# Expert layers of a two-block network: 64 of 256 tokens take their chosen table rows by indirect transfers, the dense products run over the other 192

## The chip, the cores and the metric

The kernel runs on one core of one Trainium2 chip. The metric is the device time of one execution in microseconds (us), lower is better. All data and sums are float32; large products split each operand into a high part (rounded to the matmul's input format) and a low part (what is left), and add three of the four partial products.

## What is computed

```python
def _peer(x, wq, k1, k2, u_tab, v_tab):
    # 8 heads, product keys (2 x 128 sub-keys), top 16 per half, 256 candidates, final top 16, softmax
    q = (xt @ wq).reshape(T, PEER_HEADS, 2, PEER_DQ_HALF)
    s1 = jnp.einsum('thd,nd->thn', q[:, :, 0], k1); s2 = jnp.einsum('thd,nd->thn', q[:, :, 1], k2)
    v1, i1 = lax.top_k(s1, 16); v2, i2 = lax.top_k(s2, 16)
    cand = (v1[..., :, None] + v2[..., None, :]).reshape(T, PEER_HEADS, 256)
    cidx = (i1[..., :, None] * 128 + i2[..., None, :]).reshape(T, PEER_HEADS, 256)
    sc, pos = lax.top_k(cand, 16)
    eidx = jnp.take_along_axis(cidx, pos, axis=-1).reshape(T, 128)
    gate = jax.nn.softmax(sc, axis=-1).reshape(T, 128)
    ub = jnp.take(u_tab, eidx, axis=0)                       # 16384 x 1024 table
    act = gelu(jnp.einsum('td,tkd->tk', x, ub))
    vb = jnp.take(v_tab, eidx, axis=0)                       # 16384 x 1024 table
    return jnp.einsum('tk,tkd->td', gate * act, vb)
```

There are 256 tokens of width 1024. A first block of two layers (FFN, hybrid mixer, FFN) comes first and is untouched; then two layers of a mixer and this expert layer, each followed by a layer norm. Each token chooses 8 x 16 = 128 of 16,384 experts.

## The kernel before, in words

Everything is one hand-written program per engine; the order in each is written out, and engines meet at semaphores only. All weights come as one stream of 944 units of 128 x 1024 floats (512 KB each). SyncE (SP) loads unit n into one of three slots of `ring` as soon as unit n-3 has been split (`load`, L497). ScalarE (ACT) writes the high half of a unit to `wsp` and VectorE (DVE) the low half (`Splitter.one`, L446: L454 and L457); TensorE (PE) then uses it.

An expert layer (`peer` in each engine's program) goes through these stages:

- Queries and scores: 16 units, then 8 heads x 2 halves of scores for each block of 128 tokens. Block 0's scores stay in PSUM (`ACC`), block 1's are copied to `sc1`.
- **U stage**, 128 units. Unit j holds the rows of the first table whose first sub-key is j. `product_unit` (L714) makes 24 matmuls, each with a 128 x 128 piece of the table as the stationary operand and the 256 tokens moving; ACT takes the gelu (L1758), giving for each expert and token an activation. Block 0's activations stay in `arena`; block 1's are spilled to DRAM (`act_out`, L513).
- During the first 92 units (`U_FIRST`) DVE picks the experts: `first_choice` (top 16 of 128, twice a head), `pair_sums`, `second_choice` (top 16 of 256), `places`, `look_up`, `less_the_first`, `gates_of` (softmax), between which it puts its own low halves one at a time (`low_next`). GpSimd (POOL) makes 18 of the low halves (`POOL_LOWS`, L680) at the start, while DVE chooses for four heads of block 0. ACT takes the exponentials after units 19, 39 and 76 (`EXP_AT`); for each it stops until DVE has sent the scores, and no high half is made meanwhile.
- The gates of block 0's tokens go by scatter: POOL issues 128 indirect transfers (L688) that add 128 gates each into a cleared DRAM buffer, `second_dram`. The 32 groups of four tokens of block 1 (`GROUPS`) go by one-hots: DVE makes two one-hot matrices and two scaled ones (L2645, L2654), PE multiplies them (L1342, 8 matmuls a group) and ACT copies the result into `arena` (L1807). `groups_behind` puts one group behind each unit from 93 on.
- **V stage**, 128 units. SP fetches the spilled row j from DRAM (`second_back`, L527), DVE multiplies it with `arena` (`gate`, L2671), ACT and DVE split the product (L1789, L2676) and `down_unit` (L777) makes 12 matmuls with 512 columns moving: 2 blocks of tokens x 3 partial products x 2 halves of the width, summed in four PSUM banks.
- The layer norm adds the four banks to `h`, block 0 first.

DVE's program in one round of the V stage, in order: `gate(j + 1)`, `low(j)`, the low half of unit j+1.

Of the kernel before, what the change touches and what calls it, by code (L numbers as in the profile page):

```python
# [13 lines left out]
F32 = mybir.dt.float32  # L14
# [7 lines left out]
P = 128  # L22
D = 1024
# [19 lines left out]
U_FIRST = 92  # L43
POOL_LOWS = 18
EXP_AT = (19, 39, 76)
ZEROED = 16
# [3 lines left out]
GROUPS = P // 4  # L50
ROUND = 16 * TOPK
# [34 lines left out]
PEER_STAGES = [("xT", 8, 0), ("tt", 16, 16), ("score", 4, 0), ("U", U_FIRST, U_FIRST), ("selT", 1, 0),  # L86
# [3 lines left out]
def groups_behind(q):  # L90

    return min(GROUPS, max(0, q - U_FIRST))

# [21 lines left out]
def build_program(nc, x, stream, consts, consts1, levels, p1, p2, swt, wa, wgu, rows1, rows2, rows3, out):  # L115
    ctx = ExitStack()
    with ctx:
# [9 lines left out]
        arena = at("arena", 0, [P, NKEYS * T])  # L127
        ysp = at("ysp", 0, [P, 2, 4, T], F32R)
        scratch = at("scratch", 0, [P, NKEYS * T])
        place = 4 * NKEYS * T  # L130
# [15 lines left out]
        selT = at("selT", place + 8192 + 4 * 1280, [P, 4, P], F16)  # L146
        acts = at("acts", place + 8192 + 4 * 1536, [P, 4, P])
# [7 lines left out]
        spots = at("spots", place + 2048, [P, HK], U32)  # L155
# [178 lines left out]
        second_dram = [nc.dram_tensor(f"second_dram{l}", (NKEYS * P * T, 1), F32, kind="Internal").ap() for l in range(DEPTH)]  # L334
        second_rows = [d.rearrange("(j p t) o -> j p (t o)", j=NKEYS, p=P) for d in second_dram]
        row_dram = [nc.dram_tensor(f"row_dram{l}", (4, T), F32, kind="Internal").ap() for l in range(DEPTH)]
        rows_out = sem("rows_out")
        bm_in = sem("bm_in")
        zeroed = sem("zeroed")
        scattered = sem("scattered")  # L340
# [7 lines left out]
        gated = sem("gated")  # L348
        high_done = sem("high_done")
# [139 lines left out]
        def _(sp):  # L489
# [2364 lines left out]
```

## Time and profile before

| | us |
|---|---|
| median of 3 runs (2989.09 to 2989.77) | 2989.67 |
| the profiled execution | 2988.89 |
| its span | 2986.9 |
| PE busy in the span | 2928.5 |
| DVE busy | 2124.6 |
| ACT busy | 1498.2 |
| POOL busy | 680.0 |

Times in the trace are counted from the start of the span. The second expert layer's U stage starts at 2237.06 and its V stage at 2626.11; the first one's at 1325.26 and 1714.19. "Idle before" an instruction is the time that its engine stood still ahead of it. A time in brackets with an arrow in a timeline is such a wait and what ended it. In the timelines a row may merge several instructions: its count is behind the x, its second number the time from the first one's start to the last one's end. Engine SPq is SyncE's queue of transfers. PEld is the weight load that goes ahead of each matmul. In a windows row the columns are: length, then busy time and number of instructions of PE, PEld, DVE, ACT and POOL, the granted clock of PE (1.00 is 2.4 GHz), the busy share of the 16 DMA engines and GB/s.

### The profile page before, as it was taken

How to read it: one execution, taken by the hardware profiler on the slowest of the kernel's cores; microseconds unless marked ns; L12 is line 12 of the kernel's file. 1: busy time of each engine (PE TensorE's matmuls, PEld its weight loads, DVE VectorE, ACT ScalarE, POOL GpSimd, SP SyncE). 2: the span in 40 equal slices, each digit the busy share in tenths (PEclk: the TensorE clock that was granted, in tenths of full speed). 3: DMA queues.
4: the chain of work that ended last, by engine and by line, in shares of the span. 5: the costliest groups of instructions: out<-in, count | busy, mean ns of one | idle time of the engine just before them, and what ended most of it. 6: DMA issues, size and time to landing. Idle time of an engine off the chain costs nothing.

```text
span 2986.9 us, 54746 instructions
## 1 busy us (share of the span) xinstructions
PE 2928.5 (98%) x18452; PEld 2598.6 (87%) x18452; DVE 2124.6 (71%) x3656; ACT 1498.2 (50%) x2410; POOL 680.0 (23%) x443
## 2 busy tenths in 40 slices
PE   8999999999999999999999999999999999999998
PEld 7888888888878888899999988888899999988887
DVE  6667566766766667758986677777758996767776
ACT  4455444444554445445555544455545555554544
POOL 0002100000021002117877400000207877500000
PEclk9998999999999999999999999999999999999999
DMA  6545455555473554457887677776446888777775
GB/s 222 190 161 180 153 167 186 174 183 189 148 233 113 184 187 152 157 173 199 198 211 189 176 247 262 243 240 203 163 163 191 196 209 197 176 235 266 239 244 189
DMA packets 255982, 581.52 MB, mean 195 GB/s; under 512 B 61336, under 2 KB 127168, under 8 KB 255344
## 3 DMA queue, kind: packets, MB, share of 16 engines
q1 hardware_dynamic: 210656, 547.94, 56.8%
q0 software_dynamic: 45200, 31.93, 6.9%
q8 instruction: 76, 1.25, 0.2%
q14 instruction: 50, 0.41, 0.0%
HBM read 542.92 MB, written 36.84 MB: 194 GB/s over the span
## 4 chain that ended last, share of the span: by engine, by line
PE 81%; DVE 10%; ACT 4%; issue 2%; DMA 2%; POOL 1%; SPq 0%; DVEq 0%; ACTq 0%
PE acc L785 31%; PE work L721 26%; PE work L731 9%; PE work L733 5%; DVE wsp L457 4%; PE acc L1205 2%; PE acc L849 2%; ACT wsp L454 2%; DMA ring<-in_stream 2%; PE acc L1342 1%; ACT scratch L1421 1%; PE work L1127 0%; POOL st L584 0%; DVE scratch L2033 0%; PE work L1242 0%
## 5 line engine op out<-in xcount | busy, mean ns | idle before, releaser
L457 DVE TENSOR_TENSOR wsp<-ring,wsp 128x1024 fp32r<-128x1024 f32 x908 | 1105.2, 1225 | 568.7 <-ACT wsp L454 564.4
L454 ACT ACTIVATE wsp<-ring 128x1024 fp32r<-128x1024 f32 x944 | 984.9, 1052 | 506.1 <-PE work L721 251.8
L721 PE MATMUL work<-xsp,wsp 128*128 128x256 f32 x7872 | 971.7, 285 | 6.2 <-DVE wsp L457 3.2
L721 PEld LDWEIGHTS work<-xsp,wsp 128*128 128x128 f32 x7872 | 953.8, 192 | 11.2 <-DVE wsp L457 4.5
L785 PE MATMUL acc<-wsp,hsp 128*128 128x512 f32 x4128 | 955.4, 390 | 6.6 <-DVE hsp L2676 4.7
L785 PEld LDWEIGHTS acc<-wsp,hsp 128*128 128x128 f32 x4128 | 767.8, 188 | 171.1 <-issue 4.4
L731 PE MATMUL work<-xsp,wsp 128*128 128x512 f32 x1408 | 503.7, 400 | 6.5 <-DVE xsp L1861 5.0
L688 POOL DMA_INDIRECT second_dram<-rows_sb,spots x256 | 465.8, 1819 | 148.4 <-issue 90.8
L733 PE MATMUL work<-xsp,wsp 128*128 128x256 f32 x1408 | 395.8, 281 | 0.0
L731 PEld LDWEIGHTS work<-xsp,wsp 128*128 128x128 f32 x1408 | 265.4, 188 | 74.6 <-DVE xsp L1861 6.1
L584 POOL TENSOR_TENSOR st<-st,mhalf 128x1 f32<-128x1 f32 x24 | 20.6, 862 | 1356.4 <-DVE st L1881 805.0
L1789 ACT ACTIVATE hsp<-arena 128x256 fp32r (+1 forms) x256 | 107.0, 418 | 336.4 <-PE acc L785 322.7
L733 PEld LDWEIGHTS work<-xsp,wsp 128*128 128x128 f32 x1408 | 266.7, 189 | 3.1
L2676 DVE TENSOR_TENSOR hsp<-arena,hsp 128x256 fp32r<-128x256 f32 x256 | 108.8, 425 | 60.1 <-ACT hsp L1789 60.0
L1456 ACT ACTIVATE hsp<-scratch 128x256 fp32r<-128x256 f32 x88 | 36.8, 418 | 218.4 <-DVE scratch L1954 218.4
L1448 ACT ACTIVATE scratch<-scratch 128x256 f32<-128x256 f32 x88 | 36.8, 418 | 188.1 <-DVE scratch L1944 188.1
L680 POOL TENSOR_TENSOR wsp<-ring,wsp 128x1024 fp32r<-128x1024 f32 x36 | 89.7, 2492 | 130.6 <-ACT wsp L454 130.4
L2671 DVE TENSOR_TENSOR arena<-arena,back 128x256 f32 (+1 forms) x256 | 107.2, 419 | 10.5 <-ACT arena L1807 6.0
L849 PE MATMUL acc<-wsp,xsp 128*128 128x512 f32 x384 | 100.8, 413 | 0.0
L1205 PE MATMUL acc<-wsp,xsp 128*128 128x512 f32 x384 | 93.9, 397 | 0.0
L849 PEld LDWEIGHTS acc<-wsp,xsp 128*128 128x128 f32 x384 | 72.9, 197 | 16.2
L1205 PEld LDWEIGHTS acc<-wsp,xsp 128*128 128x128 f32 x384 | 70.3, 188 | 15.3
(355 smaller groups left out, 2138.1 us busy)
## 6 DMA issues: line engine op xcount, KB each, us to landing
ring<-in_stream SPq DMA_DIRECT2D x944, 512.0 KB
back<-second_dram SPq DMA_DIRECT2D x256, 128.0 KB, 3.2
second_dram<-back POOLq DMA_DIRECT2D x32, 512.0 KB, 13.3
second_dram<-arena SPq DMA_DIRECT2D x184, 64.0 KB
rows_sb<-in_rows POOLq DMA_DIRECT2D x10, 512.0 KB, 6.4
second_dram<-acts SPq DMA_DIRECT2D x72, 64.0 KB
second_dram<-rows_sb,spots POOLq DMA_INDIRECT x256
h_saved_dram<-h POOLq DMA_DIRECT2D x2, 1024.0 KB, 5.0
```

Source lines behind the costliest of these rows:

```text
L454: self.eng.activation(dst[:, 0, :], src, ACT.Copy).then_inc(high_done, 1)
L457: self.eng.tensor_tensor(dst[:, 1, :], src, dst[:, 0, :].bitcast(F32), ALU.subtract)\
L688: pool.indirect_dma_start(out=second_dram[l], in_=selv[:, 0, 2, n:n + 1], in_offset=None, out_offset=bass.IndirectOffsetOnAxis(spots[:, n: ...
L721: mm = pe.matmul(out_, lhsT=w[:, a, 128 * c:128 * c + 128], rhs=xsp[:, b, c, :], start=(c == 0 and n == 0), stop=(c == DC - 1 and n == 2))
L731: pe.matmul(out_, lhsT=w[:, 0, 128 * c:128 * c + 128], rhs=xcs[:, c, :, :].rearrange("p s t -> p (s t)"), start=(c == 0), stop=False)
L733: mm = pe.matmul(out_[:, 0:T], lhsT=w[:, 1, 128 * c:128 * c + 128], rhs=xsp[:, 0, c, :], start=False, stop=(c == DC - 1))
L785: mm = pe.matmul(ACC[2 * b + n][:, :], lhsT=act[:, pa, 128 * b:128 * b + 128], rhs=w[:, pw, 512 * n:512 * n + 512], start=(first and m == ...
L849: mm = pe.matmul(ACC[2 * (g % 2) + b][:, :], lhsT=xsp[:, px, c, 128 * b:128 * b + 128], rhs=w[:, pw, 512 * cc:512 * cc + 512], start=(c == ...
L1205: mm = pe.matmul(ACC[2 * (g % 2) + b][:, :], lhsT=xsp[:, px, c, 128 * b:128 * b + 128], rhs=w[:, pw, 512 * cc:512 * cc + 512], start=(c == ...
L1789: act.activation(hsp[:, j % 2, 0, :], arena[:, bass.ds(it * (6 * T) + j * T, T)], ACT.Copy)\
L2671: tt(a, a, back[j % 4], ALU.mult).then_inc(gated, 1)
L2676: tt(hsp[:, j % 2, 1, :], arena[:, bass.ds(it * (12 * T) + j * T, T)], hsp[:, j % 2, 0, :].bitcast(F32), ALU.subtract).then_inc(act_low, 1)
```

## The change

Of block 1's 128 tokens the last 64 are taken out of the dense products. For each of them, 64 rows at a time on each half of the 128 partitions, POOL fetches the chosen rows of the first table by indirect transfers from a copy of it in row order (`urows`, a new input), DVE takes the inner product of each row with the token's `h` (a `scalar_tensor_tensor` with a sum, L2663), ACT takes the gelu, DVE multiplies with the gates, POOL fetches the rows of the second table (straight from the stream) and DVE adds each, scaled, to a sum (L2684). A partition holds one of the 64 tokens and 64 of its 128 experts: 64 transfers of 128 rows x 4 KB for each table and layer, through 6 slots. At the end PE adds the two halves with a small matrix, `fold`.

The other 192 tokens (`TD`): the U products are 192 columns wide and all activations are spilled. All gates of the 192 go by one-hots, 48 groups in place of 32, five groups behind every two units from unit 61 on; the scatter and the clearing of its buffer go. POOL makes the low halves of 69 units in place of 18, and DVE none during the choice. In a V unit the 64 tokens of block 1 that are left have their high and low parts side by side as 128 stationary columns: 4 matmuls for them (all four partial products) and 6 for block 0, 10 in place of 12.

```diff
-U_FIRST = 92
-POOL_LOWS = 18
-EXP_AT = (19, 39, 76)
+U_FIRST = 60
+POOL_LOWS = 69
+DOTS_FROM = 76
+EXP_AT = (19, 36, 56)
-GROUPS = P // 4
+GROUPS = (T - 64) // 4
+FETCHED = 64
+TD = T - FETCHED
+PAIRS_OF = TOPK // 2
+SLOTS = 6
+ROWS = PH * PAIRS_OF
+AHEAD = 4
+COEF_AT = (106, 127)
 def groups_behind(q):
-    return min(GROUPS, max(0, q - U_FIRST))
+    return min(GROUPS, max(0, 5 * (q - U_FIRST) // 2))
+def dots_behind(q):
+    return min(ROWS, max(0, ROWS * (q - DOTS_FROM) // (NKEYS - 2 - DOTS_FROM)))
...
 # POOL
-                pool.wait_ge(zeroed, 16 * ZEROED * (l + 1))
-                for i in range(PH):
-                    ...
-                        pool.indirect_dma_start(out=second_dram[l], in_=selv[:, 0, 2, n:n + 1], in_offset=None,
-                                                out_offset=bass.IndirectOffsetOnAxis(spots[:, n:n + 1], 0),
-                                                compute_op=ALU.add).then_inc(scattered, 16)
+                def fetch(n):
+                    m = n % ROWS
+                    k = TOPK * (m // PAIRS_OF) + m % PAIRS_OF
+                    if 2 * ROWS * l + n >= SLOTS:
+                        pool.wait_ge(row_used, 2 * ROWS * l + max(n - SLOTS + 1, 0))
+                    table, which = (urows, 0) if n < ROWS else (value_rows, 1)
+                    pool.indirect_dma_start(out=fetched[:, n % SLOTS, :], out_offset=None, in_=table,
+                                            in_offset=bass.IndirectOffsetOnAxis(gidx[:, which, k:k + 1], 0))\
+                        .then_inc(row_in[n % SLOTS], 16)
...
+                for n in range(2 * ROWS):
+                    fetch(n)
...
 # PE, U stage
-                        product_unit(G, q, G.bank(q)[:, 0:T], it * UNITS_BODY)
+                        product_unit(G, q, G.bank(q)[:, 0:TD], it * UNITS_BODY, n_=TD)
 # PE, value_unit
-                    down_unit(G, i, hsp[:, i % 2, :, :], first, last, 6 * n)
+                    for m in range(2):
+                        for n in range(2):
+                            mm = pe.matmul(ACC[2 + n][:, :], lhsT=both[:, 2 * P:2 * TD], rhs=w[:, m, 512 * n:512 * n + 512],
+                                           start=(first and m == 0), stop=(last and m == 1))
+                    ...
+                    for m, n in order:
+                        pa, pw = PARTS[m]
+                        mm = pe.matmul(ACC[n][:, :], lhsT=act[:, 0:P, pa], rhs=w[:, pw, 512 * n:512 * n + 512],
+                                       start=(first and m == 0), stop=(last and m == 2))
...
+                pe.wait_ge(row_used, 2 * ROWS * (l + 1))
+                for n in range(2):
+                    pe.wait_ge(packed_out, 2 * l + n + 1)
+                    c = slice(512 * n, 512 * n + 512)
+                    pe.matmul(ACC[2 + n][:, :], lhsT=fold[:, 64:192], rhs=row_total[:, c], start=True, stop=False)
+                    mm = pe.matmul(ACC[2 + n][:, :], lhsT=fold[:, 0:P], rhs=packed[:, c], start=False, stop=True)
...
 # DVE
+                def dots(n):
+                    for _ in range(n):
+                        m = taken[0]
+                        r = row(m)
+                        ...
+                        stt(r, r, 1.0, xrow, ALU.mult, ALU.mult, accum_out=coef[:, m:m + 1]).then_inc(row_used, 1)
+                        taken[0] += 1
...
-                for q in range(U_FIRST + 1, NKEYS - 2):
+                for q in range(U_FIRST + 1, NKEYS):
                     for g in range(groups_behind(q - 1), groups_behind(q)):
                         if g + 1 < GROUPS:
                             one_hot(g + 1)
                         gate_parts(g)
-                    split.upto(U.u + q + 1)
+                    if q < NKEYS - 2:
+                        if split.next == U.u + 3 + POOL_LOWS and U.u + q + 1 >= split.next:
+                            dve.wait_ge(low_done, split.next)
+                        split.upto(U.u + q + 1)
+                    dots(dots_behind(q) - taken[0])
...
+                coefficients(0)
+                for m in range(AHEAD):
+                    add_row(m)
...
                     for j in range(2, 14):
                         gate(j + 1, it)
                         low(j, it)
                         split.one(V.u + j + 1, it, 12)
+                        if j % 2:
+                            add_row(AHEAD + (j - 3) // 2, it)
```

DVE where the one-hots begin, behind the last unit of the choice. Before, one group stands ahead of each low half:

```order
L2632 MEMSET st 128x1
L2645 TENSOR_TENSOR one_hots<-iota_65,selT 128x512 x4
L2654 TENSOR_TENSOR one_hots<-one_hots,selT 128x512 x2
L457 TENSOR_TENSOR wsp<-ring,wsp 128x1024
L2645 TENSOR_TENSOR one_hots<-iota_65,selT 128x512 x2
L2654 TENSOR_TENSOR one_hots<-one_hots,selT 128x512 x2
L457 TENSOR_TENSOR wsp<-ring,wsp 128x1024
```

In the changed kernel the same place reads:

```order
L2755 MEMSET st 128x1
L2769 TENSOR_TENSOR one_hots<-iota_71,selT 128x512 x4
L2778 TENSOR_TENSOR one_hots<-one_hots,selT 128x512 x2
L2769 TENSOR_TENSOR one_hots<-iota_71,selT 128x512 x2
L2778 TENSOR_TENSOR one_hots<-one_hots,selT 128x512 x2
L2769 TENSOR_TENSOR one_hots<-iota_71,selT 128x512 x2
L2778 TENSOR_TENSOR one_hots<-one_hots,selT 128x512 x2
```

DVE's low halves are gone from between the groups; while these 27 groups run, POOL makes them.

POOL from the saving of `h` on. Before, it makes 18 low halves in six rounds of three and then issues the scatter:

```order
L680 TENSOR_TENSOR wsp<-ring,wsp 128x1024
L676 REGISTER_ALU
L676 COMPARE_AND_BRANCH
L688 DMA second_dram<-rows_sb,spots 4194304x1 x128
L694 DMA h<-h_saved_dram 128x2048
```

In the changed kernel 23 rounds come first, and all transfers wait behind them:

```order
L710 TENSOR_TENSOR wsp<-ring,wsp 128x1024
L706 REGISTER_ALU
L706 COMPARE_AND_BRANCH
L731 DMA gidx<-gidx 64x4x8 x4
L736 DMA fgate<-fgate 64x4x8 x2
L723 DMA fetched<-in_urows,gidx 128x1024 x64
L723 DMA fetched<-in_stream,gidx 128x1024 x25
L742 DMA h<-h_saved_dram 128x2048
L723 DMA fetched<-in_stream,gidx 128x1024 x39
```

No indirect transfer writes DRAM any more, and 128 now write SBUF.

DVE in two units of the V stage of the changed kernel, where each unit had `arena<-arena,back`, `hsp<-arena,hsp` and `wsp<-ring,wsp` before:

```order
L2799 TENSOR_TENSOR arena<-arena,back_61 128x192
L2803 REGISTER_ALU
L2804 TENSOR_TENSOR gsp<-arena,gsp 128x192
L491 REGISTER_ALU
L492 TENSOR_TENSOR wsp<-ring,wsp 128x1024
L2797 REGISTER_ALU
L2799 ISA
L2799 TENSOR_TENSOR arena<-arena,back_87 128x192
L2803 REGISTER_ALU
L2804 TENSOR_TENSOR gsp<-arena,gsp 128x192
L491 REGISTER_ALU
L492 TENSOR_TENSOR wsp<-ring,wsp 128x1024
L2679 REGISTER_ALU
L2684 ISA
L2684 SCALAR_TENSOR_TENSOR xrow<-fetched,coef,xrow 128x1024
```

The last row is the addition of a fetched row, behind every second unit.

## Rows read from the trace of the kernel before

**Rows 1.** The page: busy time by engine, and the chain that ended last.

```profile
PE 2928.5 (98%) x18452; PEld 2598.6 (87%) x18452; DVE 2124.6 (71%) x3656; ACT 1498.2 (50%) x2410; POOL 680.0 (23%) x443
...
PE 81%; DVE 10%; ACT 4%; issue 2%; DMA 2%; POOL 1%; SPq 0%; DVEq 0%; ACTq 0%
```

**Rows 2.** Windows: the first 92 units of the second U stage; 200 us of V.

```profile
2237.06:2499.60 262.54, 260.91 (x2163) 259.77 (x2162) 218.49 (x512) 136.49 (x195) 201.83 (x104) 1.00 0.77 198
...
2750.00:2950.00 200.00, 200.00 (x884) 165.60 (x883) 146.28 (x221) 100.11 (x147) 0.00 (x0) 1.00 0.73 242
```

**Rows 3.** Timeline of PE: U stage, V stage and next stage of the first layer begin.

```profile
1325.26 4.92 PE L721 MATMUL work<-xsp,wsp 128*128 128x256 f32 x39
...
1714.19 2.00 PE L785 MATMUL acc<-wsp,hsp 128*128 128x512 f32 x8
...
2066.20 1.07 PE L743 MATMUL work<-xsp 128*128 128x512 f32 x4
```

**Rows 4.** Timelines of PEld and PE: trains of weight loads and matmuls; one group by shape.

```profile
234.50 1.86 PEld L897 LDWEIGHTS work<-cst,scratch 128*128 128x128 f32 x16
...
L897 PE MATMUL work<-cst,scratch 128*128 128x1 f32 x64 | 7.4, 245 | 0.0
...
1325.23 4.86 PEld L721 LDWEIGHTS work<-xsp,wsp 128*128 128x128 f32 x40
...
2849.83 6.96 PE L785 MATMUL acc<-wsp,hsp 128*128 128x512 f32 x30
...
1664.23 0.63 PE L1342 MATMUL acc<-one_hots 128*128 128x128 f16 x8
```

**Rows 5.** Timeline of DVE in the choice beside POOL's lows (layer 2); durations of L2504, L680.

```profile
2238.07 0.30 DVE L2474 MAX8 topv<-acc 128x8 f32<-128x128 f32 x1 [5.29 <-ACT scores L1751]
...
2239.93 0.30 DVE L2474 MAX8 topv<-acc 128x8 f32<-128x128 f32 x1
...
2256.45 0.43 DVE L2474 MAX8 rows_sb<-rows_sb 128x8 f32<-128x256 f32 x1
...
2258.97 0.43 DVE L2474 MAX8 rows_sb<-rows_sb 128x8 f32<-128x256 f32 x1
...
2281.91 2.28 DVE L2564 TENSOR_SCALAR spots<-rows_sb,pr 128x64 uint32<-128x64 f32 x1
...
L2504 DVE TENSOR_TENSOR rows_sb<-topv x8: 1218/1219/3476, 1341.1 to 2418.3; 128x1024 f32<-128x1024 f32 x8
...
L680 POOL TENSOR_TENSOR wsp<-ring,wsp x36: 2394/2401/2873, 1329.6 to 2290.4; 128x1024 fp32r<-128x1024 f32 x36
```

**Rows 6.** Timeline of ACT at the third exponential.

```profile
2460.99 1.28 ACT L1763 ACT_TABLE_LOAD   x1
2462.28 0.31 ACT L1763 ACTIVATE rows_sb<-rows_sb 128x128 f32<-128x128 f32 x1
...
2463.90 1.06 ACT L454 ACTIVATE wsp<-ring 128x1024 fp32r<-128x1024 f32 x1
```

**Rows 7.** Timeline of DVE and ACT: one group of one-hots in the first layer.

```profile
1664.90 0.76 DVE L2645 TENSOR_TENSOR one_hots<-iota,selT 128x512 f16<-128x512 f16 x2 [0.83 <-PE acc L1342]
...
1665.58 0.75 DVE L2654 TENSOR_TENSOR one_hots<-one_hots,selT 128x512 f16<-128x512 f16 x2
```

**Rows 8.** Timeline of DVE in one unit of the V stage.

```profile
2850.84 1.23 DVE L457 TENSOR_TENSOR wsp<-ring,wsp 128x1024 fp32r<-128x1024 f32 x1 [0.53 <-ACT wsp L454]
...
2851.98 0.42 DVE L2671 TENSOR_TENSOR arena<-arena,back 128x256 f32 x1
...
2852.61 0.43 DVE L2676 TENSOR_TENSOR hsp<-arena,hsp 128x256 fp32r<-128x256 f32 x1 [0.21 <-ACT hsp L1789]
```

**Rows 9.** Windows with much DMA; durations of the indirect transfers' issue and of L2332.

```profile
5.00:10.00 5.00, 2.26 (x11) 2.29 (x12) 3.11 (x7) 3.45 (x9) 3.28 (x5) 1.00 1.04 409
...
2722.00:2742.00 20.00, 20.00 (x89) 16.33 (x87) 12.91 (x19) 8.63 (x13) 1.73 (x3) 1.00 0.89 311
...
L688 POOL DMA_INDIRECT second_dram<-rows_sb,spots x256: 1537/1581/2631, 1390.3 to 2595.1; - x128
...
L2332 DVE SCALAR_TENSOR_TENSOR h<-h,st,rows_sb x10: 1279/1282/1286, 1155.4 to 2981.2; 128x1024 f32<-128x1024 f32 x10
```

More of the change, by code:

```diff
@@ L348, in build_program @@
         gated = sem("gated")
+        xrow_in = sem("xrow_in")
+        rows_moved = sem("rows_moved")
+        gates_moved = sem("gates_moved")
+        row_in = [sem(f"row_in{i}") for i in range(SLOTS)]
+        row_used = sem("row_used")
+        packed_out = sem("packed_out")
         high_done = sem("high_done")
@@ L671, in _ @@
                 pool.wait_ge(h_saved, 16 * (l + 1))
+                for half in range(2):
+                    pool.dma_start(xrow[64 * half:64 * half + 64, :], saved[64:P, 1, :]).then_inc(xrow_in, 16)
                 U = Group(f"peer{l}", "U")
@@ new lines, in _ @@
+                for half in range(2):
+                    i = half * (PH // 2)
+                    pool.wait_ge(ev("rows_known"), 2 * l + half + 1)
+                    for w in range(2):
+                        pool.dma_start(first_half(gidx[0:64, w, :], i), second_half(gidx[64:P, w, :], i)).then_inc(rows_moved, 16)
+                pool.wait_ge(rows_moved, 64 * (l + 1))
+                pool.wait_ge(ev("sel_ready"), 3 * l + 2)
+                for half in range(2):
+                    i = half * (PH // 2)
+                    pool.dma_start(first_half(fgate[0:64, :], i), second_half(fgate[64:P, :], i)).then_inc(gates_moved, 16)
@@ L1767, in activate_all @@
                     rounds = (last - first) // UNITS_BODY
-                    with act.Fori(0, rounds) as it:
-                        for q in range(first, first + UNITS_BODY):
-                            activate(q, it)
+                    if rounds > 1:
+                        with act.Fori(0, rounds) as it:
+                            for q in range(first, first + UNITS_BODY):
+                                activate(q, it)
+                    else:
+                        rounds = 0
                     for q in range(first + rounds * UNITS_BODY, last):
@@ L1819, in peer @@
                     split.upto(G.u + j + 1)
+                act.wait_ge(ev("packed_done"), l + 1)
+                act.wait_ge(row_used, 2 * ROWS * (l + 1))
+                for n in range(2):
+                    act.activation(packed[:, 512 * n:512 * n + 512], ACC[2 + n][:, :], ACT.Copy).then_inc(packed_out, 1)
                 split.upto(G.u + 129)
@@ L2606, in peer @@
                 for half in range(2):
-                    low_next()
                     pair_sums(half)
                     for i in range(PH // 2 * half, PH // 2 * (half + 1)):
-                        low_next()
-                        second_choice(1, i, low_next if i % 2 else None)
-                    if half == 0:
-                        for i in range(PH // 2, PH):
-                            for m in range(2):
-                                low_next()
-                                first_choice(1, i, m)
```

216 lines of the change are left out of this document (138 added, 78 removed).

## The prediction

> **What bounds the kernel now.** I read the page first: PE is busy 98% of the span and stands for 81% of the chain that ended last [rows 1]. The windows tell the stages apart [rows 2]: in the first 92 units of U, PE and its weight loads are both full (260.9 and 259.8 of 262.5 us) and POOL and DVE have work most of the time; in V, PE is full while DVE has 146 of 200 us and the DMA engines 0.73 of their time, at 242 GB/s. So before the change PE sets both stages, and the question is what stands right behind it. In the first layer U takes 1325.26 to 1714.19, 388.9 us, and V from there to 2066.20, 352.0 us [rows 3].
>
> Rates of PE come from trains of equal instructions, their time less one instruction's, over their number less one [rows 4]. A U matmul (256 columns) starts every (4.86 - 0.19) / 39 = 0.120 us, so a unit of 24 takes 2.88. A V matmul (512 columns) starts every (6.96 - 0.39) / 29 = 0.2265, so a unit of 12 takes 2.72. A one-hot group of 8 takes, from (0.63 - 0.22) / 7, 0.06 each and some 0.52 in all with its joints.
>
> **The change part by part**, per expert layer.
>
> *(a) Units 0 to 59.* The U matmuls go from 256 to 192 columns. That would be 0.09 us if columns were all, but in [rows 4] the 16 matmuls of one column behind 128-column weight loads still start every (1.86 - 0.19) / 15 = 0.111 us. So a unit costs between 24 x 0.111 = 2.67 and the 2.88 of now; I take 2.67, as the weight load is the same. The Trainium skill ("TensorE: Matmul & The Clock Gate", section "LDWEIGHTS (loading the stationary operand)") gives columns / 1.2 ns, 107 ns for 128, which would make it 2.56; the trace is near it, a little above.
>
> That gain isn't had, because DVE is late. Its choice is on the way: ACT stops after unit 56 until DVE has sent the last scores, and makes no high half meanwhile. Prices from [rows 5]: `first_choice` 2239.93 - 2238.07 = 1.86, `second_choice` 2258.97 - 2256.45 = 2.52; the first four heads of block 0 with all around them, beside POOL's low halves, 2238.07 to 2284.19 = 46.1. In these, some DVE instructions take over 2 us longer than alone: L2504 takes 1.22 alone and 3.48 beside an L680, whose own length is 2.40, and L2564 2.28. DVE waits there for POOL's instruction to end. Now POOL makes 69 low halves, so all of the choice is priced that way. The two halves of block 0 cost 46.1 and one more conversion of 2.3 each (the second index), 96.8. Block 1: 16 x 1.86 + 8 x 2.52 + 2 x 3.5 (L2504) = 57.0, and the look-ups: in the half above they are 46.1 - 14.9 - 10.1 - 3.5 - 2.3 = 15.3, with the same instructions at twice the size here, between 15 and 30, taken as 17 since most of it is waiting. Three softmaxes about 1 each. With a start at 1.0 the scores are sent at 175. Then a table load, the exponential, a table load, a high half (1.28 + 0.31 + 1.28 + 1.06 [rows 6]) and POOL's low half 2.40: unit 59 starts at 181, unit 60 at 184. Before it started at 60 x 2.88 = 172.8. **+11 us.** If the 17 is 30, or if DVE is not held up at all, this is +24 or -7 (60 units of 2.67 and the exponential).
>
> *(b) Units 60 to 79.* All 48 groups fall here, 2.5 a unit. A group takes DVE four instructions in (0.76 + 0.75), 1.51 us [rows 7]: 72.4. DVE's own low halves of the units from 72 on cost 1.14 each (L457 starts, L2671 starts 1.14 later [rows 8]): 8 x 1.14 = 9.1. Three inner products, 1.24 each (L2332 is of that form, 1.28 [rows 9]): 3.7. The transposed choice and the start 4. That is 89, against PE's 20 x 2.67 + 48 x 0.52 = 78. Until unit 71 POOL still makes low halves, nine of 2.40 = 21.6 us. No row of before shows a one-hot beside one. If they go side by side it costs nothing; if they exclude each other, all 21.6. I take all, by the row that is nearest, L2504, also a `tensor_tensor` with both inputs in SBUF. 111, against 20 x 2.88 = 57.6: **+53**, down to +32.
>
> The Trainium skill ("SBUF — State Buffer", section "Who interferes with whom") says that a DVE instruction with two SBUF inputs and a GpSimd instruction that reads SBUF exclude each other for a whole instruction. L2504's row agrees.
>
> *(c) Units 80 to 127 and the handover.* PE has 48 x 2.67 = 128. DVE has 48 low halves and 61 inner products, 48 x 1.14 + 61 x 1.24 = 130. The DMA engines: the fullest window moves 409 GB/s at a share of 1.04 [rows 9], so 512 KB cost at least 1.28 us. 48 loads and 61 fetches (each 128 rows of 4 KB, 512 KB) are 139.5, the spills of 96 KB 0.24 each, 11.5: 151 us. So here the transfers set the pace. POOL's issue takes 1.6 (up to 2.6) with 0.3 between [rows 9], 61 x 2.1 = 128, hidden. At the end DVE has the last inner products and four row additions (4 x 1.2, each waiting for a fetch) ahead of the low half of unit 127; PE has two units of work in hand, so some 9 us are lost. 160, against 48 x 2.88 + 32 x 0.52 = 154.9: **+5**.
>
> *(d) V.* PE's unit becomes 10 x 0.2265 = 2.27. DVE per unit: 1.14 for the low half, 0.28 and 0.28 for the two instructions of 192 columns (0.42 at 256, which start 0.33 apart, less a quarter of the streaming), and half a row addition of 1.2: 2.30. The DMA engines: 1.5 x 1.28 + 0.24 for the row read back = 2.16. Three resources stand within 6% of each other, and DVE, which waited 0.53 and 0.21 for ACT in each unit of before [rows 8], has no slack left to take a wait. The floor is 2.30, the ceiling what (c)'s slower DMA would give, 2.75. I take 2.50, a third of DVE's waits back. 128 x (2.50 - 2.72): **-28**.
>
> *(e) Ends.* Four matmuls of `fold`, plain float32 of 512 columns, between 0.45 and 0.9 each (two instructions, in one or two passes), behind two copies by ACT that hide under the last unit; six more transposes. **+4**, 2 to 6. The scatter and the clearing of its buffer lay beside PE's work: 0; the 1 to 3 us that they could hide aren't in the sum.
>
> Sum: 11 + 53 + 5 - 28 + 4 = +45 a layer, **+90 us**. Against the profiled execution's 2988.9 this is **3079**; the median of the runs, 2989.7, lies 0.8 above it. A measurement of this kernel can tell 0.2%, some 6 us, from no change.
>
> **The rivals.**
> - *V at its floor, DVE and POOL side by side* (faster). (a) -7, (b) +32, (c) +5, (d) 128 x (2.30 - 2.72) = -54, (e) +4: -20 a layer, 2949. It decides where DVE's wait for POOL doesn't come with the one-hots and a V unit is under 2.45. For it: PE was the only full engine in V. Against it: L2504's row. 0.12.
> - *V at its floor, the waits as forecast.* 11 + 53 + 5 - 54 + 4 = +19: 3027. 0.18.
> - *Side by side, V at 2.50.* +6 a layer: 3001. 0.10.
> - *Transfers slower than their best.* The only window in which POOL's queue moves megabytes beside the stream shows 311 GB/s at 0.89 [rows 9], 350 when full: 512 KB in 1.50. (c) 109 x 1.50 + 48 x 0.28 + 9 = 186, +31; V 2.75, +4: 103 a layer, 3195. 0.15.
> - The forecast, 0.45.
>
> **How the numbers follow.** Faster by over 0.2% is the first rival, 0.12, and a hundredth for what I don't see. Within 0.2% 0.02. Slower, the rest, 0.85. The range leaves out the first rival and goes up to the last: 2990 to 3195. The slower cases are near enough to each other that they need no range of their own.
>
> **What would show it.** In the changed profile: U matmuls 0.111 apart in the first units; ACT idle ahead of the third exponential for over 10 us, ended by DVE, and PE idle with it; from unit 61 to 71 one-hot instructions of over 2 us beside POOL's low halves, and units of 6 us; DMA share near 1 from unit 80 on, DVE waiting for fetched rows, units of 3.1 us; V units of 2.3 to 2.75. U in all 455 us (184 + 111 + 160), V 320. I am wrong if U takes under 420, which would mean that DVE and POOL don't hold each other up, or if V units stay above 2.72.

## The result, and the profile after

The changed kernel takes 3172.9 us (median of 4 runs, 3162.6 to 3185.5), the one before 2989.4: a ratio of 1.0616, 95% interval 1.0571 to 1.0661, or +183.5 us. The forecast was +90 and 3079. The direction and the range (2990 to 3195) hold, the size is off by a factor of two. The profiled execution took 3166.1, its span is 3164.3.

The page of the changed kernel, busy time by engine and the chain that ended last, as in [rows 1]:

```profile
PE 2901.0 (92%) x18218; PEld 2535.7 (80%) x18218; DVE 2364.2 (75%) x4093; ACT 1482.7 (47%) x2364; POOL 801.7 (25%) x528
...
PE 44%; DMA 17%; DVE 16%; issue 10%; POOL 7%; ACT 6%; DVEq 1%; SPq 0%; POOLq 0%; ACTq 0%
```

PE's busy time fell by only 27 us, and PE no longer makes up the chain: it was 81% of it, now 44%. The windows tell where. Five stretches of the first expert layer (columns as in [rows 2]):

```profile
1321.28:1500.20 178.92, 166.22 (x1449) 164.83 (x1447) 156.69 (x451) 84.62 (x129) 145.99 (x59) 0.96 0.67 202
1500.20:1550.00 49.80, 36.34 (x282) 34.63 (x280) 37.41 (x67) 17.23 (x30) 19.41 (x8) 0.76 0.34 102
1550.00:1624.70 74.70, 60.47 (x577) 57.38 (x577) 62.36 (x146) 32.76 (x59) 17.26 (x17) 0.89 0.48 149
...
1700.00:1791.16 91.16, 71.34 (x587) 69.07 (x587) 72.10 (x96) 33.28 (x54) 48.53 (x37) 0.93 1.03 403
...
1900.00:2050.00 150.00, 131.31 (x532) 101.82 (x531) 122.23 (x184) 73.06 (x107) 40.09 (x30) 0.98 0.93 322
```

In the second and third stretch, units 60 to 79, no engine is full, and PE's clock is down. In the fourth the DMA engines are full. In the last, in V, PE, DVE and the DMA engines are all at 0.8 to 0.93, and none is full.

The places where the stages begin, in the timeline of PE:

```profile
1321.28 70.17 PE L769 MATMUL work<-xsp,wsp 128*128 128x192 f32 x624
1392.18 62.90 PE L769 MATMUL work<-xsp,wsp 128*128 128x192 f32 x552 [0.73 <-POOL wsp L710]
...
1494.28 5.36 PE L769 MATMUL work<-xsp,wsp 128*128 128x192 f32 x24 [11.09 <-POOL wsp L710]
...
1500.22 5.60 PE L769 MATMUL work<-xsp,wsp 128*128 128x192 f32 x48
...
1624.69 2.90 PE L769 MATMUL work<-xsp,wsp 128*128 128x192 f32 x24 [0.59 <-DVE wsp L492]
...
1791.16 1.94 PE L1409 MATMUL acc<-wsp,gsp 128*128 128x512 f32 x4
...
2150.57 1.02 PE L1434 MATMUL acc<-xrow,fold 128*128 128x512 f32 x2
...
2153.60 5.15 PE L791 MATMUL work<-xsp 128*128 128x512 f32 x20
```

The first row holds 26 units in 1392.18 - 0.73 - 1321.28 = 70.2, 2.70 a unit. 1500.22 is the start of unit 60, 1624.69 that of unit 80, 1791.16 that of V, 2150.57 that of the fold. The stages, in us a layer:

| | forecast | first layer | second layer |
|---|---|---|---|
| units 0 to 59 | 184 | 178.9 | 181.2 |
| units 60 to 79 | 111 | 124.5 | 123.2 |
| units 80 to 127 and handover | 160 | 166.5 | 164.1 |
| V | 320 | 359.4 | 357.7 |
| fold | 4 with all else | 3.0 | 3.4 |

The first layer takes 2153.60 - 1321.28 = 832.3 where it took 740.9 [rows 3]: +91.4, and twice that is the result. The forecast had +45. To set its terms against the measured ones, the stages of the kernel before have to be read from the same trace, by counting PE's matmuls: units 0 to 59 took 176.0, units 60 to 79 57.7, units 80 to 127 155.2 and V 352.0. The sum of the prediction goes from 172.8, 57.6, 154.9 and 348.2 (128 x 2.72), 7 us less in all, so its stage times (779 with the fold) lie 53 below the 832 and its difference 46 below the +91. In differences, for the first layer:

| | forecast | measured | missing |
|---|---|---|---|
| units 0 to 59 | +11 | +2.9 | -8 |
| units 60 to 79 | +53 | +66.8 | +14 |
| units 80 to 127 and handover | +5 | +11.3 | +6 |
| V | -28 | +7.4 | +35 |
| fold | +4 | +3.0 | -1 |

So V is 35 of the 46 us a layer that the forecast lacked: it was to give 28 back and costs 7 more. Units 60 to 79 are 14, and the other three nearly cancel.

### The profile page after: what moved, and what is told of

Read it like the earlier page. It is cut to its first block, busy times and chain, and to the rows that moved or that the text cites. A ratio compares the mean times of both kernels' runs of the same rounds, so it can differ in the third digit from the quotient of the medians.

```text
span 3164.3 us, 54654 instructions
## 1 busy us (share of the span) xinstructions
PE 2901.0 (92%) x18218; PEld 2535.7 (80%) x18218; DVE 2364.2 (75%) x4093; ACT 1482.7 (47%) x2364; POOL 801.7 (25%) x528
## 4 chain that ended last, share of the span: by engine, by line
PE 44%; DMA 17%; DVE 16%; issue 10%; POOL 7%; ACT 6%; DVEq 1%; SPq 0%; POOLq 0%; ACTq 0%
DMA ring<-in_stream 16%; PE acc L833 9%; PE work L779 9%; PE work L769 9%; POOL wsp L710 6%; DVE wsp L492 6%; PE work L781 5%; ACT wsp L489 4%; PE acc L1253 2%; PE acc L897 2%; PE acc L1416 2%; DVE one_hots L2778 2%; DVE one_hots L2769 2%; PE acc L1409 1%; DVE fetched L2663 1%
## 5 line engine op out<-in xcount | busy, mean ns | idle before, releaser
L769 PE MATMUL work<-xsp,wsp 128*128 128x192 f32 (+1 forms) x7872 | 966.9, 284 | 88.2 <-DVE wsp L492 59.6
L1416 PE MATMUL acc<-wsp,gsp 128*128 128x512 f32 x1536 | 411.6, 404 | 0.0
L710 POOL TENSOR_TENSOR wsp<-ring,wsp 128x1024 fp32r<-128x1024 f32 x138 | 340.6, 2475 | 243.5 <-ACT wsp L489 243.2
L781 PE MATMUL work<-xsp,wsp 128*128 128x256 f32 x1408 | 395.8, 281 | 0.0
L1409 PE MATMUL acc<-wsp,gsp 128*128 128x512 f32 x1024 | 293.5, 409 | 82.9 <-DVE gsp L2804 82.5
L1416 PEld LDWEIGHTS acc<-wsp,gsp 128*128 128x128 f32 x1536 | 305.5, 199 | 63.8
L1409 PEld LDWEIGHTS acc<-wsp,gsp 128*128 128x128 f32 x1024 | 190.7, 193 | 156.8 <-issue 114.8
L723 POOL DMA_INDIRECT fetched<-in_stream,gidx x128 | 183.5, 1434 | 458.3 <-DVE xrow L2684 429.9
L833 PE MATMUL acc<-wsp,hsp 128*128 128x512 f32 x1056 | 256.8, 392 | 1.9 <-DVE hsp L2047 1.9
L833 PEld LDWEIGHTS acc<-wsp,hsp 128*128 128x128 f32 x1056 | 191.9, 188 | 44.3 <-DVE hsp L2047 3.6
L723 POOL DMA_INDIRECT fetched<-in_urows,gidx x128 | 172.2, 1345 | 217.9 <-DVE fetched L2663 200.2
L2684 DVE SCALAR_TENSOR_TENSOR xrow<-fetched,coef,xrow 128x1024 f32<-128x1024 f32 x126 | 161.2, 1279 | 4.2 <-DMA fetched<-in_stream,gidx 4.0
L2663 DVE SCALAR_TENSOR_TENSOR fetched<-fetched,xrow 128x1024 f32<-128x1024 f32 x128 | 153.7, 1218 | 0.0
```

The costliest lines, as they stand in the source:

```text
L710: pool.tensor_tensor(dst[:, 1, :], ring[:, n % RING, :], dst[:, 0, :].bitcast(F32), ALU.subtract) .then_inc(low_done, 1)
L723: pool.indirect_dma_start(out=fetched[:, n % SLOTS, :], out_offset=None, in_=table, in_offset=bass.IndirectOffsetOnAxis(gidx[:, which, k:k ...
L769: mm = pe.matmul(out_, lhsT=w[:, a, 128 * c:128 * c + 128], rhs=xsp[:, b, c, 0:n_], start=(c == 0 and n == 0), stop=(c == DC - 1 and n == 2))
L781: mm = pe.matmul(out_[:, 0:T], lhsT=w[:, 1, 128 * c:128 * c + 128], rhs=xsp[:, 0, c, :], start=False, stop=(c == DC - 1))
L833: mm = pe.matmul(ACC[2 * b + n][:, :], lhsT=act[:, pa, 128 * b:128 * b + 128], rhs=w[:, pw, 512 * n:512 * n + 512], start=(first and m == ...
L1409: mm = pe.matmul(ACC[2 + n][:, :], lhsT=both[:, 2 * P:2 * TD], rhs=w[:, m, 512 * n:512 * n + 512], start=(first and m == 0), stop=(last an ...
```

## The experiments

The table has the stages of each run's profiled execution, mean of the two layers, and the run's median time. The ratio's interval is given with each. Executions of the changed kernel and its variants scatter more than those of the kernel before (23 us between four of the changed kernel), and the profiled one is not always near the median: with 60 low halves on POOL it is the slowest of five, 3143.5.

| kernel | units 60 to 79 | 80 to 127 | V, a unit | us |
|---|---|---|---|---|
| changed | 124 | 165 | 2.80 | 3172.9 |
| second table's fetches small | 122 | 169 | 2.50 | 3085.0 |
| the same by plain transfers | 121 | 167 | 2.76 | 3152.7 |
| row additions narrow | 121 | 168 | 2.68 | 3136.7 |
| 60 low halves on POOL | 103 | 170 | 2.81 | 3121.3 |
| first table's fetches small | 122 | 143 | 2.80 | 3121.2 |
| small fetches, narrow additions | 123 | 167 | 2.39 | 3061.5 |
| idle matmuls ahead of groups | 124 | 168 | 2.79 | 3179.5 |
| groups and products spread | 69 | 172 | 2.80 | 3079.2 |
| spread, addition first | 71 | 175 | 2.93 | 3105.0 |
| spread, weights' low half first | 72 | 174 | 3.08 | 3151.5 |
| spread, gates one further ahead | 70 | 174 | 2.87 | 3090.0 |

Theory after the result: V is paced by the loop of the three ring slots. A load can start only when DVE has made the low half of the unit three before it, and now it lands later, since a fetch is in flight beside it. The rival is DVE, with a row addition in every second unit. The chain of waits of the changed kernel in V, a piece of it (start, us, what):

```profile
1861.02 6.02 DMA ring<-in_stream
1867.06 1.07 ACT wsp L489
...
1869.29 0.47 DVE xrow L2684
...
1870.49 0.35 DVE arena L2799
1870.84 0.27 DVE gsp L2804
1871.11 1.15 DVE wsp L492
1872.42 6.43 DMA ring<-in_stream
1878.87 1.07 ACT wsp L489
```

In the 1872.42 - 1861.02 = 11.4 us from one load's start to the other's, SP starts four loads, so this is four units of 2.85; 6.0 of them pass until the load has landed, and the rest is one high half and what DVE does up to the second low half behind it. That this loop sets the pace is a reading of the chain. The experiments below test it.

**1. Small fetches in V.**

```diff
-pool.indirect_dma_start(out=fetched[:, n % SLOTS, :], out_offset=None, in_=table,
+w = D if n < ROWS + SLOTS else 32
+if w == 32:
+    table = stream.rearrange("n p (a d) -> (n p a) d", d=32)
+pool.indirect_dma_start(out=fetched[:, n % SLOTS, 0:w], out_offset=None, in_=table,
```

> The second table's fetches, all but a layer's first six, move 128 bytes a row and not 4 KB (so 16 KB and not 512 KB each; the rows are then not the chosen ones and only 32 of 1024 columns of them are fresh). All instructions of the engines stay. Theory 'transfers': the V stage is paced by the loop of three ring slots, whose load lands later because a fetch is in flight beside it. Then the load lands within 4.5 us and a V unit falls from 2.80 us to what DVE takes, 2.3 to 2.5: V 295 to 320 us a layer, the kernel about 3060 to 3100. Rival 'DVE': the row additions make DVE late. Then V stays at 345 us or more a layer and the kernel above 3150.

Measured: 3085.0, ratio 1.0306 (1.0286 to 1.0327); V 318.9 and 320.7 a layer, 2.50 a unit. Windows of V:

```profile
1900.00:2050.00 150.00, 146.28 (x608) 115.55 (x607) 141.03 (x213) 82.50 (x123) 41.08 (x30) 0.99 0.80 258
2900.00:3050.00 150.00, 146.13 (x607) 115.15 (x606) 140.95 (x215) 81.19 (x121) 40.74 (x30) 0.99 0.82 265
```

DVE is now at 0.94 and PE at 0.97, and the chain's loads land in 4.35 to 4.73 us in place of 5.4 to 7.2. So the bytes of the fetches cost 0.30 us a unit, 39 us a layer. What is left, 2.50, is what the forecast took for V with the fetches in it.

**2. The same bytes by plain transfers.**

```diff
+if n >= ROWS:
+    pool.dma_start(fetched[:, n % SLOTS, :], stream[n]).then_inc(row_in[n % SLOTS], 16)
+    return
```

> Each fetch of the second table is replaced by one plain transfer of the same 512 KB from the stream, from the same queue into the same slot (other rows, the same bytes and semaphores). If V is paced by the bytes that the transfers share, nothing moves: 3160 to 3185. If it is the form of the fetches (one row per descriptor at scattered addresses, and GpSimd's 1.4 us of issue), a V unit falls towards that of the run with small fetches, and the kernel under 3130.

Measured: 3152.7, ratio 1.0545 (1.0523 to 1.0567), V 2.76 a unit. It is 20 us below the changed kernel, a little outside what was expected for "bytes", and far from the 3130 of "form". So the bytes make nearly all of it. The 0.04 of 0.30 a unit that would be the form's is hardly clear of the scatter of the runs.

**3. Row additions on 32 columns.**

```diff
-ins = stt(row_total, fetched[:, s, :], c, row_total, ALU.mult, ALU.add)
+ins = stt(row_total[:, 0:32], fetched[:, s, 0:32], c, row_total[:, 0:32], ALU.mult, ALU.add)
```

> The row additions of the V stage work on 32 of 1024 columns (the sum over the fetched rows is left out for the rest); all transfers stay. DVE sheds 60 x about 1.1 us a layer. Theory 'transfers': a V unit stays within 0.15 of 2.80 us, the kernel 3130 to 3175. Rival 'DVE': a V unit falls to PE's 2.27 to 2.4, V to 290 to 307 us a layer, and the kernel to 3050 to 3070.

Measured: 3136.7, ratio 1.0482 (1.0458 to 1.0506), V 2.68 a unit. DVE fell from 122 to 102 of 150 us, and the DMA share rose to 0.96. So DVE's load alone isn't the bound: with the additions all but gone and the fetches as they were, V stays above 2.6. The additions cost 0.12 a unit.

**4. Sixty low halves on POOL** (`POOL_LOWS = 60`, was 69).

> POOL makes the low halves of 60 units in place of 69, DVE those from unit 63 on. Theory 'POOL and DVE exclude each other in the one-hots': nine low halves of 2.40 us on POOL that hold DVE up become nine of 1.14 on DVE, so units 60 to 79 fall from 124 us by 8 to 15 a layer, and no one-hot takes over 2 us from unit 63 on: the kernel 3140 to 3160. Rival 'it is PE's lower clock after its idle time and the ping-pong with the one-hots': units 60 to 79 stay within 5 us of 124, the kernel 3165 to 3185. Rival 'side by side': DVE gets nine more instructions, +10 a layer, 3190.

Measured: 3121.3, ratio 1.0445 (1.0427 to 1.0462). Units 60 to 79 take 102.1 and 104.8. What an instruction of the one-hots takes there, in the changed kernel:

```profile
L2778 DVE TENSOR_TENSOR one_hots<-one_hots,selT x94: 406/418/2604, 1504.5 to 1623.0; 128x512 f16<-128x512 f16 x94
```

and with 60 low halves on POOL:

```profile
L2778 DVE TENSOR_TENSOR one_hots<-one_hots,selT x94: 407/415/448, 1507.0 to 1603.6; 128x512 f16<-128x512 f16 x94
```

The longest falls from 2604 to 448 ns when POOL's low halves are gone. In the changed kernel's first layer POOL makes ten low halves behind unit 60's start; each has just one long one-hot instruction beside it, which ends 0.3 us after it: the first, which starts in the middle of POOL's, is 1.81 us long, the others are 2.56 to 2.63. The exclusion of the two engines is shown. Nine low halves moved from POOL to DVE are worth 20 us a layer, more than the 8 to 15 expected, and the kernel is faster than expected too. These 20 are not all DVE's: its busy time in the stretch falls by 10 only (99.8 to 90.0 in the first layer), and PE's granted clock rises with it, from 0.76 and 0.89 to 0.95:

```profile
1505.00:1605.00 100.00, 84.31 (x850) 79.95 (x849) 88.15 (x212) 47.81 (x85) 12.59 (x15) 0.95 0.50 155
```

**5. Small fetches of the first table.** The edit of experiment 1, for `SLOTS <= n < ROWS` and on `urows`.

> The first table's fetches, all but a layer's first six, move 128 bytes a row and not 4 KB (other rows, and only 32 of 1024 columns fresh); everything else as changed. Theory 'transfers' of the prediction: units 80 to 127 with the handover (166 us a layer in the changed kernel, DMA share 1.0) fall to what DVE takes, 130 + 9 to 150: the kernel 16 to 27 us a layer faster, 3120 to 3145. Rival 'DVE and PE, coupled through two shallow buffers': this stretch stays at 160 or more, the kernel above 3155. V stays at 2.80 a unit in both.

Measured: 3121.2, ratio 1.0443 (1.0419 to 1.0467). Units 80 to 127 take 143.2 and 142.7 in place of 165. The window from 1630 to 1780:

```profile
1630.00:1780.00 150.00, 138.05 (x1182) 136.02 (x1180) 136.38 (x189) 64.32 (x106) 115.83 (x66) 0.95 0.84 252
```

The bytes of the fetches cost 22 us in this stretch, so the transfers were its bound. Behind them stand PE and DVE, both at 0.9, and POOL's issuing, which is 49% of the chain of waits there: so 143 is not DVE's own pace.

**6. Both of V's costs away** (edits 1 and 3).

> Small second-table fetches and row additions on 32 columns together. With the transfers gone alone a V unit took 2.49, with the additions gone alone 2.68. If PE is the next bound, 2.27 to 2.35 a unit, V 290 to 300 us a layer, the kernel 3040 to 3060. If something else is in the loop (ACT, the fetch of the spilled row, the ring of three slots), it stays above 2.40, V above 307, the kernel above 3065.

Measured: 3061.5, ratio 1.0239 (1.0222 to 1.0256), V 2.39 a unit. PE in V:

```profile
1952.28 1.08 PE L1412 MATMUL acc<-wsp,gsp 128*128 128x512 f32 x4
1953.19 1.56 PE L1419 MATMUL acc<-wsp,gsp 128*128 128x512 f32 x6
1954.59 1.08 PE L1412 MATMUL acc<-wsp,gsp 128*128 128x512 f32 x4
```

Between 1900 and 2050 PE never waits (busy 150.0 of 150), and a unit takes 1954.59 - 1952.28 = 2.31. So PE is the bound, at 2.31 in an undisturbed stretch and 2.39 over the whole stage, a little above the 2.35 that was expected of PE; 10 x 0.2265 was 2.27. The row of six starts its matmuls (1.56 - 0.39) / 5 = 0.234 apart, against 0.2265 in [rows 4].

**7. Idle matmuls ahead of each group.** In the changed kernel units 60 to 79 show something that was not in the forecast. Timelines of PE, then of DVE and POOL:

```profile
1510.93 1.03 PE L1394 MATMUL acc<-one_hots 128*128 128x128 f16 x8 [2.86 <-DVE one_hots L2778]
1511.72 5.16 PE L769 MATMUL work<-xsp,wsp 128*128 128x192 f32 x24
...
1521.82 5.23 PE L769 MATMUL work<-xsp,wsp 128*128 128x192 f32 x24
```

```profile
1504.38 2.38 POOL L710 TENSOR_TENSOR wsp<-ring,wsp 128x1024 fp32r<-128x1024 f32 x1 [1.14 <-ACT wsp L489]
1504.45 2.93 DVE L2778 TENSOR_TENSOR one_hots<-one_hots,selT 128x512 f16<-128x512 f16 x2
...
1507.05 2.53 POOL L710 TENSOR_TENSOR wsp<-ring,wsp 128x1024 fp32r<-128x1024 f32 x1 [0.30 <-ACT wsp L489]
1507.30 2.90 DVE L2769 TENSOR_TENSOR one_hots<-iota,selT 128x512 f16<-128x512 f16 x2
...
1517.39 0.76 DVE L2769 TENSOR_TENSOR one_hots<-iota,selT 128x512 f16<-128x512 f16 x2 [3.84 <-PE acc L1394]
```

POOL makes DVE late, PE stands still 2.86 us for DVE, then runs its next 24 matmuls in 5.16 us and not 2.90 (the lower of its clock's two levels; the window's mean is 0.76), and DVE in turn stands still 3.84 us for PE, since only three groups' one-hots fit. The edit gives PE work in its idle time:

```diff
+for _ in range(3):
+    pe.matmul(ACC[g % 4][:, :], lhsT=xsp[:, 0, 6, 0:128],
+              rhs=xcs[:, 4, :, :].rearrange("p s t -> p (s t)"), start=True, stop=True)
 pe.wait_ge(oh_ready, n + 1)
```

The wait for the group's bank, which stood behind `oh_ready`, goes ahead of both.

> PE makes three idle 512-column matmuls of 0.2265 us ahead of each one-hot group (into the group's own bank, overwritten after), 33 us a layer of PE work with no use, where it waits for DVE anyway. If PE's lower clock after its idle time costs time in units 60 to 79, the granted clock there rises from 0.76 to 0.89 to above 0.95, the 24 matmuls of a unit take 2.9 and not 5.2 us, and the stretch falls from 124 us to 110 to 120 in spite of the added work. If DVE, held up by POOL, sets it alone, it stays within 4 of 124. If PE is the bound, it rises to 135 or more.

Measured: 3179.5, ratio 1.0648 (1.0626 to 1.0669), and 124.2 in both layers for units 60 to 79:

```profile
1500.00:1550.00 50.00, 44.79 (x360) 39.11 (x360) 39.86 (x78) 18.57 (x31) 20.98 (x9) 0.91 0.38 121
1550.00:1624.00 74.00, 71.04 (x629) 60.75 (x629) 56.38 (x131) 31.63 (x54) 18.55 (x16) 1.00 0.44 135
```

The clock rose to 0.91 and 1.00 (above 0.95 was expected), the time did not fall. The 33 us of added work a layer cost nothing, but PE is then nearly full itself (71.0 of 74.0), so the run doesn't say how much the lower clock cost. That stays open.

**8. Groups and inner products spread over the stage.**

```diff
-POOL_LOWS = 69
-DOTS_FROM = 76
+POOL_LOWS = 60
+DOTS_FROM = 64
-    return min(GROUPS, max(0, 5 * (q - U_FIRST) // 2))
+    return min(GROUPS, max(0, q - U_FIRST))
```

> One one-hot group behind each unit from 61 to 108 in place of five behind every two, the inner products from unit 65 on in place of 77, and POOL makes 60 low halves in place of 69. DVE has 48 groups of 1.51, 65 low halves of 1.14 and 64 inner products of 1.24 = 226 us behind unit 60, PE 68 x 2.67 + 48 x 0.52 = 207. If DVE's total is what bounds the second half of U, units 60 to 127 take 230 to 250 us a layer where the kernel with 60 low halves on POOL took 273, and the kernel 3060 to 3100. If it is the coupling inside each unit, 260 or more, and the kernel 3110 or more.

Measured: 3079.2, ratio 1.0308 (1.029 to 1.0325). Units 60 to 127 take 241 and 242 a layer, where they took 291 and 287 in the changed kernel and 270 to 277 in experiment 4. The window from 1510 to 1700:

```profile
1510.00:1700.00 190.00, 178.23 (x1694) 172.00 (x1693) 184.97 (x339) 91.23 (x156) 59.22 (x58) 1.00 0.94 333
```

DVE is busy 185.0 of 190 us, with no wait for PE but one of 0.6, and the clock is whole. It is the fastest complete version of this study, and 89 us slower than the kernel before. The second half of U is then close to DVE's sum (226 expected, 225.5 busy of 241.1 in the first layer), with the DMA engines nearly as full beside it (0.94), and V is as it was.

**9 and 10. The order in DVE's round of V.** The loop suggests that what stands ahead of the low half of the weights should go. In the changed kernel DVE waits there with an addition behind it:

```profile
1911.17 1.23 DVE L492 TENSOR_TENSOR wsp<-ring,wsp 128x1024 fp32r<-128x1024 f32 x1 [3.10 <-ACT wsp L489]
1912.31 1.28 DVE L2684 SCALAR_TENSOR_TENSOR xrow<-fetched,coef,xrow 128x1024 f32<-128x1024 f32 x1
...
1918.35 1.22 DVE L492 TENSOR_TENSOR wsp<-ring,wsp 128x1024 fp32r<-128x1024 f32 x1 [2.42 <-ACT wsp L489]
```

```diff
+if j % 2:
+    add_row(AHEAD + (j - 3) // 2, it)
 split.one(V.u + j + 1, it, 12)
-if j % 2:
-    add_row(AHEAD + (j - 3) // 2, it)
```

> The kernel with the spread groups (3079), and in V DVE adds the fetched row before it waits for the unit's high half and not after its low half. In the changed kernel DVE stood still 2.2 to 3.1 us every few units ahead of a low half, with a ready row addition of 1.20 behind it. Theory 'loop of three ring slots, lengthened by what stands in DVE's order between a landing and the low half': the addition fills the wait, the low half comes up to 1.2 us sooner in every second unit, a V unit falls from 2.80 to 2.55 to 2.70, the kernel to 3047 to 3066. Rival 'the transfers are simply at their capacity in V': within 0.05 of 2.80, the kernel 3070 to 3088. It can be worse where the fetched row lands late: then DVE waits for that row with the low half behind it, 2.85 or more a unit.

Measured: 3105.0, ratio 1.036 (1.0314 to 1.0407), V 2.93 a unit: worse by 0.13, a miss (one of its four runs took 3079.6, the others 3101.8 to 3112.1). It isn't worse for the reason that the expectation names, since no wait of DVE for a fetched row is among that kernel's waits in V. The other order:

```diff
+split.one(V.u + j + 1, it, 12)
 gate(j + 1, it)
 low(j, it)
-split.one(V.u + j + 1, it, 12)
```

> As above, but DVE makes the low half of the next unit of weights first in each round, before the two instructions on the activations (0.27 each) and the row addition. By the theory of the loop the ring slot comes free 0.5 us sooner in a round and a V unit falls to 2.60 to 2.75. Against it: PE's unit then waits until the next unit's weights have landed, so PE has one unit less in hand: 2.85 or more a unit. By 'capacity' within 0.05 of 2.80.

Measured: 3151.5, ratio 1.0546 (1.0528 to 1.0563), V 3.08 a unit. The waits of that kernel from 1850 to 2050 (us in total, times, longest):

```profile
ACT gsp L1868 <- DVE arena L2799: 111.4, 64, 1.8
PEld acc L1409 <- DVE wsp L492: 61.8, 65, 2.6
...
ACT wsp L489 <- DMA ring<-in_stream: 3.3, 3, 1.5
```

and those of the changed kernel from 1850 to 2100:

```profile
POOL fetched L723 <- DVE xrow L2684: 162.0, 39, 6.1
ACT wsp L489 <- DMA ring<-in_stream: 47.4, 47, 3.1
...
ACT gsp L1868 <- DVE arena L2799: 33.8, 24, 3.1
```

With the weights' low half first, ACT hardly waits for a load any more (3.3 us in 200, before 47.4 in 250): the ring's loop is loose. But now the activations come too late, and PE has a unit less in hand. In both orders the DMA share fell, to 0.84 and 0.82. So V is not simply at the transfers' capacity: it changes by 10% with the order of the same work. An addition ahead of a low half also delays that low half where DVE was not waiting, and this seems to weigh more than the waits it fills: with the addition first, PE's weight loads wait 43.9 us of 200 for DVE's low half, a wait that the kernel with the spread groups doesn't have. That account was made after the result and is not tested.

**11. Gates one unit further ahead**, with the original place of the addition.

```diff
-gate(j + 1, it)
 low(j, it)
 split.one(V.u + j + 1, it, 12)
+gate(j + 2, it)
```

The first and the last units are changed to match.

> The kernel with the spread groups (3079), and in V DVE multiplies the gates of a unit one unit further ahead: the round is low half of the activations, low half of the weights, product with the gates of the unit after next, row addition. ACT no longer waits for the product (20 us of 200 in the spread kernel, 111 in the one with the weights' low half first), the low half of the weights stands 0.27 us earlier behind its landing, and PE keeps its unit in hand. By the loop theory a V unit falls from 2.80 to 2.60 to 2.75, the kernel to 3040 to 3070. If it is only the row addition ahead of the next low half that counts (1.20 us, in every second round), it stays at 2.75 to 2.85 and the kernel at 3070 to 3088.

Measured: 3090.0, ratio 1.036 (1.0331 to 1.0389), V 2.87: a third miss, 0.07 above. No order that was tried is better than the one that the change has, and the theory of the loop forecast a gain each time. So it is not shown as the account of V. A fourth ring slot, the direct test of the loop's depth, was not tried: it would need room from the six slots of fetched rows.

## Why the prediction was right or wrong

- **(a) Units 0 to 59: right.** 2.70 a unit in the first row of PE's timeline, forecast 2.67: 0.112 a matmul at 192 columns, next to the 0.111 at one column in [rows 4], so the columns are not what holds U. The choice was late by less than forecast; unit 60 starts at 178.9 and 181.2 (184), and PE stands still 11.1 us at the third exponential, about as forecast.
- **(b) Units 60 to 79: the mechanism right, 13 us too short.** That DVE and POOL exclude each other, taken from L2504 alone, is shown by experiment 4 (2604 to 448 ns). The Trainium skill ("SBUF — State Buffer", section "Who interferes with whom") says it of a DVE instruction with two SBUF inputs beside a GpSimd instruction that reads SBUF, and the one-hots, with both inputs in SBUF, agree. The price was right too: nine one-hot instructions of some 2.6 us and not 0.41 are 20 us, where the sum had 21.6; and by the same terms the kernel with 60 low halves on POOL would take 111 - 21.6 + 9 x 1.14 = 100, where it took 103. What the sum lacked is PE behind DVE. It took DVE for full, but DVE is busy 99.8 of the 124.5 us and stands still 24.5 in nine waits for PE, whose clock has fallen: with three groups in hand each waits for the other. How much of that is the clock's stays open (experiment 7).
- **(c) Units 80 to 127: right, 4 to 7 us too short.** The transfers set the pace: 403 GB/s at a share of 1.03 against the 409 of the sum, and experiment 5 takes 22 us off. The wait fell elsewhere than forecast: ACT waited for loads of the ring, 97.6 us between 1625 and 1791, and DVE for fetched rows only 3.0. The "slow transfers" rival had this stretch at 186.
- **(d) V: the step that failed.** It is "I take 2.50, a third of DVE's waits back", between a floor of 2.30 and a ceiling of 2.75. V takes 2.81 and 2.79 a unit, over the ceiling and over the 2.72 that the prediction named as a sign of being wrong. Two of the busy times behind the step were sound: PE 2.31 (2.27 forecast), DVE 1.14 + 2 x 0.27 + 0.60 = 2.28 (2.30). The third was a best case: 2.16 for the transfers takes the full 409 GB/s, but in V they moved 322 at a share of 0.93, which is 2.60 us of their busy time in a unit of 2.80 (a share that isn't quite the part of their capacity, see the last section).

  What failed is how the three were put together. The step took for the stage little more than the largest of three nearly equal costs, as if the others hid behind it. Experiments 1, 3 and 6 show that they add up: with both all but gone 2.39, with the additions 2.50, with the fetches 2.68, with both 2.80, and 2.39 + 0.11 + 0.29 is 2.79. The forecast of 2.50 is what V takes without the bytes of the fetches. Before, PE was the one full engine, and waits of the others were free.

  Why they add up is open. The loop of the ring is a reading of the chain whose three forecasts missed (experiments 9 to 11). The transfers' capacity alone doesn't explain it either: the same engines reach 403 GB/s in U, in single slices of 5 us in V they move between 183 and 414, and other orders of V move less. PE's clock has a small part that no experiment separates. Its granted mean in V is 0.94 to 0.98, which by an estimate, (1 - 0.97) x 2.80, is up to 0.08 us a unit, and in one unit behind a wait of 1.83 us four matmuls took 1.92 and the next six 2.44, in place of 1.08 and 1.56.

  The ceiling doesn't follow from its source. With 350 GB/s, (d)'s sum is 1.5 x 1.50 + 0.28 = 2.53 and not 2.75, so that the last rival's V unit comes near the measured one, and its 3195 near the 3173, is luck; its price for units 80 to 127 was 20 us too high.
- **(e) Ends: right.** The fold takes 3.0 and 3.4.

A reader of [rows 8] could have seen it: DVE waited 0.74 us of each 2.72 on ACT. The forecast asked how much of that wait was left, not what is paid when PE, DVE and the transfers each wait for the other.

## What to carry to other kernels

Where a change brings three resources near each other and the buffers between them are two or three deep, the stage costs well more than the largest of them (here 2.80 against 2.31). In this case what each of the other two brought on top of the full engine (0.11 and 0.29) added up, and a forecast near the largest missed it. Four kernels tell such costs apart: with both, without the one, without the other, without either. A walk through the loop of the buffers named what is in it, but the three reorderings chosen by it made the kernel slower.

An instruction handed to GpSimd is paid by VectorE where both work on SBUF: a low half cost 1.14 us on DVE, and on POOL it made one DVE instruction up to 2.2 us longer (2.6 in place of 0.41).

And work is better spread at a rate that every engine keeps up with: one group a unit instead of 2.5, with the same instructions, took the second half of U from 273 to 241 us a layer in the profiled executions (experiments 4 and 8). By the medians of the runs, 3121.3 and 3079.2, it is 21 us a layer.

## What the runs showed of the hardware

- PE's clock fell to the lower of its levels behind waits of 2.86 us in U (24 matmuls took 5.16 and 5.23 us in place of 2.90) and of 1.83 in V. With idle matmuls in U's waits the granted clock rose from 0.76 and 0.89 to 0.91 and 1.00.
- 512-column matmuls whose stationary operand takes every second element (the high or low parts in `gsp`) start 0.234 us apart in experiment 6, those of the kernel before 0.2265. That the stride is the cause was not tested.
- The DMA engines' busy share isn't the part of their capacity that is used: they moved 403 GB/s at 1.03, 322 at 0.93 and 198 at 0.77 [rows 2].
